# Start of a two-layer decoder step: loads split by the first chunk's needs, squares behind the raw chunks, norm sum inside block 1, products of zeros during the loads

## What is computed

```python
def rmsnorm(x, g):
    xf = x.astype(jnp.float32)
    y = xf * lax.rsqrt(jnp.mean(xf * xf, axis=-1, keepdims=True) + RMS_EPS)
    return (y * g.astype(jnp.float32)).astype(x.dtype)

def swiglu(h, w1, w3, w2):
    return (jax.nn.silu(h @ w1) * (h @ w3)) @ w2

h = rmsnorm(x, w['norm_ffn1'])
x = x + 0.5 * swiglu(h, w['ffn1_w1'], w['ffn1_w3'], w['ffn1_w2'])
...
lam = (jnp.exp(jnp.sum(w['lq1'] * w['lk1'])) - jnp.exp(jnp.sum(w['lq2'] * w['lk2'])) + lam_init)
```

## Time and profile before

| | |
|---|---|
| median of 3 runs | 2637.2 us (2636.78 to 2637.67) |
| profiled execution, own time | 2646.27 us |
| its span | 2644.4 us |
| TensorE busy | 2580.0 us (98%) |
| VectorE busy | 1793.3 us (68%) |
| ScalarE busy | 1188.8 us (45%) |
| mean granted TensorE clock | 0.992 of full |
| TensorE idle before its first product | 13.4 us |

### The profile page before, as it was taken

How to read it: one execution, slowest core, us unless ns; L and a number is a source line. 1 busy time by engine, 2 the same in 40 slices (tenths; PEclk the granted TensorE clock), 3 DMA queues, 4 the chain that set the end, 5 groups by cost and what they waited for, 6 DMA issues and landing times.

```text
span 2644.4 us, 54210 instructions
## 1 busy us (share of the span) xinstructions
PE 2580.0 (98%) x22900; PEld 2442.1 (92%) x22900; DVE 1793.3 (68%) x2307; ACT 1188.8 (45%) x1650; POOL 277.2 (10%) x150
## 2 busy tenths in 40 slices
PE   7999999999999999999999999999999999999997
PEld 7999999976699999999899999999757999999997
DVE  6887347655676798843798863567466758987346
ACT  5555223413663565532455542343236635555223
POOL 0102000331000010020001020013220000100200
PEclk9999999999999999999999999999999999999998
DMA  4233233278422233332223322322883222333221
GB/s 152 81 110 102 89 123 99 81 239 276 146 83 87 76 107 111 102 96 97 82 80 111 100 93 89 128 90 89 272 278 110 82 95 81 97 110 116 88 93 64
DMA packets 142110, 304.42 MB, mean 115 GB/s; under 512 B 14946, under 2 KB 25186, under 8 KB 141410
## 3 DMA queue, kind: packets, MB, share of 16 engines
q1 hardware_dynamic: 141922, 301.79, 34.5%
HBM read 290.30 MB, written 11.44 MB: 114 GB/s over the span
## 4 chain that ended last, share of the span: by engine, by line
PE 91%; DVE 5%; ACT 2%; DVEq 1%; issue 1%; DMA 0%; SPq 0%; ACTq 0%
PE ps L665 33%; PE ps L757 29%; PE ps L713 14%; PE ps L789 3%; PE ps L950 2%; PE ps L1042 1%; DVE ring L1944 1%; PE ps L1090 1%; PE ps L1105 1%; PE ps L1061 1%; PE ps L831 1%; PE ps L836 1%; PE ps L854 1%; PE ps L1259 1%; DVE pg L1944 0%
## 5 line engine op out<-in xcount | busy, mean ns | idle before, releaser
L665 PE MATMUL ps<-Gh,ring 128*128 128x260 f32 x2816 | 455.3, 283 | 5.9 <-DVE ring L1944 5.9
L665 PEld LDWEIGHTS ps<-Gh,ring 128*128 128x128 f32 x2816 | 387.1, 189 | 6.9 <-DVE ring L1944 6.9
L713 PE MATMUL ps<-Hh,ring 128*128 128x260 f32 x2048 | 342.3, 286 | 0.1
L1879 POOL TENSOR_TENSOR Gl<-G,Gh 128x520 fp32r<-128x520 f32 x88 | 151.2, 1740 | 1513.1 <-ACT Gh L1431 1513.1
L713 PEld LDWEIGHTS ps<-Hh,ring 128*128 128x128 f32 x2048 | 285.2, 188 | 4.3 <-issue 2.7
L665 PE MATMUL ps<-Gl,ring 128*128 128x260 f32 x1408 | 283.2, 283 | 0.0
L1944 DVE TENSOR_TENSOR ring<-rawd,ring 128x1408 fp32r<-128x1408 f32 x64 | 117.4, 1836 | 200.0 <-ACT ring L1431 200.0
L757 PE MATMUL ps<-HS,UHb 128*128 128x260 f32 x1280 | 234.3, 283 | 5.6 <-DVE ULb L1944 5.6
L757 PE MATMUL ps<-XR,UHa 128*128 128x260 f32 x1280 | 237.1, 283 | 0.0
L1431 ACT ACTIVATE ring<-raw 128x2048 fp32r<-128x2048 f32 (+1 forms) x72 | 134.3, 1866 | 227.0 <-PE ps L665 122.5
L1431 ACT ACTIVATE ring<-rawd 128x1408 fp32r<-128x1408 f32 x64 | 88.4, 1381 | 324.5 <-PE ps L665 319.7
(11 more groups left out here) (347 smaller groups left out, 5509.1 us busy)
## 6 DMA issues: line engine op xcount, KB each, us to landing
weven<-in_ffn_up SPq DMA_DIRECT2D x88, 512.0 KB, 4.7
wodd<-in_ffn_up SPq DMA_DIRECT2D x88, 512.0 KB, 4.8
rawd<-in_ffn_down SPq DMA_DIRECT2D x128, 352.0 KB, 3.5
kb<-in_cache_k SPq DMA_DIRECT2D x128, 256.0 KB, 4.2
kb<-in_cache_v SPq DMA_DIRECT2D x128, 256.0 KB, 3.9
raw<-in_w_in SPq DMA_DIRECT2D x56, 512.0 KB, 4.6
raw<-in_w_gate SPq DMA_DIRECT2D x32, 512.0 KB, 4.7
raw<-in_w_ab SPq DMA_DIRECT2D x16, 512.0 KB, 4.3
```

The lines of the kernel that those rows point to most:

```text
L665: last = nc.tensor.matmul(ps[:, bank + 2 * m + c, 0:HT], w, x[:, k0 + k, c * HT:(c + 1) * HT], start=starts and k == 0 and n == 0, stop=st ...
L713: last = nc.tensor.matmul(ps[:, 2 * m + c, 0:HT], w, x[:, k, c * HT:(c + 1) * HT], start=k == 0 and t == 0, stop=k == KD - 1 and t == 2)
L1879: nc.gpsimd.tensor_tensor(Gl[:, n, :], G0[:, n, :], Gh[:, n, :].bitcast(F32), ALU.subtract).then_inc(gl_done, 1)
```

## The change

Five edits, all at the start of layer 0's first FFN.

1. Block 0's weights go to `whole`, seven places of which four are used. The first DMA brings slots 0 and 3, those that chunk 0 needs, on a semaphore of its own; X chunks 0 and 1 follow, then slots 1 and 2 in a DMA each. ScalarE and VectorE split slots 0 and 3 ahead of raw chunk 0, and slots 1 and 2 behind it.
2. TensorE waits for the second half of block 0's split weights at chunk 1, no longer ahead of chunk 0. Later blocks wait as before.
3. All eight raw chunks are made first; the eight squares and their adds come behind them.
4. The norm sum is made inside block 1, ahead of its chunk 4, in columns 260 to 511 of banks 0 to 2, which no block uses, as three products (252, 252 and 16 columns). The root reads them with two activations. TensorE no longer waits for the root ahead of block 1.
5. VectorE clears a tile `warm`, and TensorE multiplies it with itself seven times (128 x 128 by 260 columns, fp32) ahead of block 0.

```diff
@@ def plain_parts
+            if n:
+                return WF[n % 2][q][:, 0:3:2, :], (UHa if w == 0 else ULa)[:, 2 * q:2 * q + 2, :] if n % 2 else (
+                    PWh[hid] if w == 0 else PWl[hid])[:, 2 * q:2 * q + 2, :]
+            s = (slice(0, 7, 6), slice(2, 5, 2))[q]
+            d = (slice(0, 4, 3), slice(1, 3))[q]
+            return whole[:, s, :], (PWh[hid] if w == 0 else PWl[hid])[:, d, :]
@@ up_load (SP), for block 0 of the later FFNs
+                if n == 0:
+                    s, d = ((slice(0, 4, 3), slice(0, 7, 6)), (slice(1, 3), slice(2, 5, 2)))[q]
+                    sp_.dma_start(whole[:, d, :], up[L, 0].rearrange("p (a c) -> p a c", a=4)[:, s, :]).then_inc(raw_ready[0], 16)
+                    return
@@ SP at the start
             sp_.dma_start(par[:, :], A["par"][:, 0:G_LAM]).then_inc(par_load, 16)
-            up_load(0, 0, A["ffn1_up"], 0, 0)
+            first = A["ffn1_up"][0, 0].rearrange("p (a c) -> p a c", a=4)
+            sp_.dma_start(whole[:, 0:7:6, :], first[:, 0:4:3, :]).then_inc(w_load, 16)
             x_in(0)
-            up_load(0, 0, A["ffn1_up"], 0, 1)
+            for q in range(1, 3):
+                sp_.dma_start(whole[:, 2 * q, :], first[:, q, :]).then_inc(raw_ready[0], 16)
@@ norm_sum (TensorE)
+                if L == 0 and nj == 0:
+                    for b, t in ((0, slice(0, 252)), (1, slice(252, 504)), (2, slice(504, T))):
+                        last = nc.tensor.matmul(ps[:, b, HT:HT + t.stop - t.start], ones, accu[:, t], start=True, stop=True)
+                    last.then_inc(sum_ready, 1)
+                    return
@@ up_plain (TensorE)
-                pe.wait_ge(split_done, n + (L * NB + nb + FREE + 1))
                 pe.wait_ge(evac, L * NE + n + (ub + 1))
                 for k in range(KD):
                     i, odd = divmod(k, 2)
+                    if k == (0 if n else 1):
+                        pe.wait_ge(split_done, n + (L * NB + nb + FREE + 1))
@@ ffn (TensorE)
+                def late_norm(k):
+                    if k == 4:
+                        norm_sum(L, nj)
+
                 up_plain(L, nb, ub, hid, 0, PWh[hid], PWl[hid], raw_part)
-                norm_sum(L, nj)
-                if np > 1:
-                    pe.wait_ge(rt_ready, L * NORMS + (nj + 1))
-                    for n in range(1, np):
-                        up_plain(L, nb, ub, hid, n, *((UHa, ULa) if n % 2 else (PWh[hid], PWl[hid])))
+                if np == 1:
+                    norm_sum(L, nj)
+                for n in range(1, np):
+                    up_plain(L, nb, ub, hid, n, *((UHa, ULa) if n % 2 else (PWh[hid], PWl[hid])), late_norm if n == 1 else None)
@@ TensorE, ahead of everything
+            pe.wait_ge(warm_ready, 1)
+            for n in range(7):
+                nc.tensor.matmul(ps[:, 7, 0:HT], warm[:, 0:P], warm[:, :], start=True, stop=True)
@@ norm_root (ScalarE)
+                if L == 0 and nj == 0:
+                    A_(R[:, 0:504].rearrange("p (a c) -> p a c", a=2), ps[:, 0:2, HT:512], ACT.Sqrt, scale=1.0 / D, bias=eps)
+                    A_(R[:, 504:T], ps[:, 2, HT:HT + 16], ACT.Sqrt, scale=1.0 / D, bias=eps).then_inc(rt_ready, 1)
+                    return
@@ ScalarE at the start
+            plain_high(0, 0, 0, 0, 0)
             for i in range(4):
                 act.wait_ge(x_load[i], 16)
                 if i == 0:
                     act.wait_ge(par_load, 16)
                 for m in (2 * i, 2 * i + 1):
                     raw_act(act, 0, 0, 0, m)
-                    if m < 2:
-                        plain_high(0, 0, 0, 0, m)
-                    else:
-                        square_act(act, 0, 0, m - 2)
-            for m in (KD - 2, KD - 1):
+                    if m == 0:
+                        plain_high(0, 0, 0, 0, 1)
+            for m in range(KD):
                 square_act(act, 0, 0, m)
@@ VectorE at the start
+            V.memset(warm[:, :], 0.0).then_inc(warm_ready, 1)
             V.memset(accu[:, :], 0.0)
+            plain_low(0, 0, 0, 0, 0)
+            for m in range(KD):
+                raw_dve(dve, 0, 0, 0, m)
+                if m == 0:
+                    plain_low(0, 0, 0, 0, 1)
             dve.drain()
             for m in range(KD):
-                raw_dve(dve, 0, 0, 0, m)
-                if m < 2:
-                    plain_low(0, 0, 0, 0, m)
-                else:
-                    square_dve(dve, 0, 0, m - 2)
-            for m in (KD - 2, KD - 1):
                 square_dve(dve, 0, 0, m)
```

More of the change, by code:

```diff
@@ L195, in hybrid_trunk @@
         weven = (at("weven", [P, 4, 512], F32, even_at), at("weven2", [P, 3, 512], F32, even_at + 8192))
+        whole = at("whole", [P, 7, 512], F32, even_at)
         assert even_at + 14336 <= top.at
@@ L208, in hybrid_trunk @@
         G0 = at("G0", [P, KF, T], F32, gl_at)
+        warm = at("warm", [P, HT], F32, gl_at + 20 * T * 4)
         accu = at("accu", [P, T], F32, tb_at + T * 4)
@@ L364, in hybrid_trunk @@
         VALUES = (1, 1, 1, 2, 1, 0, 1, 2, 1, 0, 1, 2, 0, 0, 0, 1, 1, 1)
-        loads, late_loads, par_load = sem("loads"), sem("late_loads"), sem("par_load")
+        loads, late_loads, par_load, w_load, warm_ready = (
+            sem(n) for n in ("loads", "late_loads", "par_load", "w_load", "warm_ready"))
         x_load = [sem(f"x_load{n}") for n in range(4)]
@@ L457, in formed, with plain_parts @@
             return sum(KF - plain(*f) for f in ((0, 0), (0, 1), (1, 0))[:2 * L + hid]) + n - plain(L, hid)
+        def plain_parts(hid, n, q, w):
+            if n:
[4 more added lines that the diff above has]
+            return whole[:, s, :], (PWh[hid] if w == 0 else PWl[hid])[:, d, :]
         def half_t(c):
@@ L1446, in plain_high @@
             def plain_high(L, nb, hid, n, q):
-                w = WF[n % 2][q]
-                to = UHa if n % 2 else PWh[hid]
-                act.wait_ge(raw_ready[n % 2], (L * NB + nb + n) // 2 * 32 + 32)
+                w, to = plain_parts(hid, n, q, 0)
+                if L or hid or n or q:
+                    act.wait_ge(raw_ready[n % 2], (L * NB + nb + n) // 2 * 32 + 32)
+                else:
+                    act.wait_ge(w_load, 16)
                 if n > 1:
                     act.wait_ge(block_done, L * NB + nb + n + 1)
-                A_(to[:, 2 * q:2 * q + 2, :], w[:, 0:3:2, :], ACT.Copy).then_inc(hi_done if q else up_hi, 1 if q else 2)
+                A_(to, w, ACT.Copy).then_inc(hi_done if q else up_hi, 1 if q else 2)
             def up_high(L, nb, hid, n, g):
@@ L1969, in plain_low @@
             def plain_low(L, nb, hid, n, q):
-                w = WF[n % 2][q]
-                h, l = (UHa, ULa) if n % 2 else (PWh[hid], PWl[hid])
+                (w, h), (w, l) = plain_parts(hid, n, q, 0), plain_parts(hid, n, q, 1)
                 if q:
@@ L1976, in plain_low @@
                     dve.wait_ge(up_hi, 2 * (up_first(L, hid) + n) + 2)
-                TT(l[:, 2 * q:2 * q + 2, :], w[:, 0:3:2, :], h[:, 2 * q:2 * q + 2, :].bitcast(F32), ALU.subtract
+                TT(l, w, h.bitcast(F32), ALU.subtract
                    ).then_inc(split_done if q else up_lo, 1 if q else 2)
```

## The result

The changed kernel takes 2645.27 us (median of 20 executions), the kernel before 2637.98 (20). The ratio is 1.0026, with a 95% interval of 1.0019 to 1.0033: 6.9 us slower, 5.0 to 8.7 (the two medians alone differ by 7.3). The direction was forecast, the size was not: 4.8 us and 2642.0 were said, with 2644.6 as the upper end. Of the 3.3 us between 2642.0 and 2645.27, 0.8 are before's own median, which was 2637.2 over 3 executions.

The account below looks back on a forecast made before the run. TensorE, busy 98%, was taken as the bound. Block 2 starting 3.2 us later plus 1.6 us of half clock in it gave 4.8 us on 2637.2, so 2642.0 us; range 2639.6 to 2644.6.

Parts of the forecast that it names:

- chunk 0 of block 0: TensorE's first chunk starts at about 9.2 us, once its half of the weights is split and X is there.
- end of the adds: VectorE's eight adds of squares, behind the raw chunks, end at 23.0 us, 0.9 sooner than 23.91.
- reciprocal: On VectorE, behind the late norm sum and root, it starts at 37.15 us instead of 29.16, 8.0 later.
- end of block 2's low parts: VectorE's PWl, queued behind the reciprocal, ends 8.26 us after the reciprocal's start; block 2 can't start without it.
- last form, behind before's: VectorE's last form, needed by TensorE at block 5, comes 4.95 us late after idle time is used up.
- The mechanism: Blocks 1 and 2 wait for ScalarE's and VectorE's chains: block 1 starts 1.4 us sooner, block 2 3.2 us later.
- The floor by VectorE's chain: At block 5, VectorE's late forms alone would make TensorE 4.5 us late, even with a cheaper second clock fall.
- The third rival: Block 1's split weights are ready when block 0 ends; block 2 starts 3.7 us sooner, 2633.5; chance 0.04.
- the term for the clock: Behind TensorE's waits before blocks 1 and 2 the clock falls to half, each fall costing 1.6 us.
- the first rival: Before's timed executions have no clock fall at block 1, so the change is 6.4 us slower, 2643.6; chance 0.2.
- a bound (2.4 of loss): Each of the two clock falls may lose 0.8 to 2.4 us, making the result +3.7 to +6.4.
- only the first 45 us or so: The part of the profiled execution that the diff was said to touch.

Follow-up runs that it names:

- Experiments 1: Changed kernel with the norm sum put back between blocks 0 and 1, still in the unused columns and without TensorE's wait for the root; ratio to before 0.9999.
- experiment 2: Kernel before with only the norm sum moved ahead of chunk 4 of block 1, in unused columns, no wait for the root; ratio 1.0017, 4.5 us.
- Experiments 5: Changed kernel with products of zeros filling TensorE's two new waits, eight ahead of block 1 and seven in its last chunk; ratio to before 1.0018.
- 7: Changed kernel with the split of block 2's weights moved ahead of the root on ScalarE and the reciprocal on VectorE; ratio to before 1.0018.
- Experiment 8: Changed kernel with block 1's weight split moved ahead of the squares and block 2's ahead of root and reciprocal; ratio to before 1.0002.
- experiment 3: Kernel before with only the eight squares and their adds moved behind all raw chunks; ratio 1.0003.
- experiment 11: Changed kernel with norm sum back between blocks 0 and 1, block 1's low parts on GpSimd, high copies between squares, lambda behind the root; ratio to before 1.0005.

## Why the prediction was right and where it was wrong

| step | said | profile |
|---|---|---|
| chunk 0 of block 0 | 9.2 | 10.54 |
| end of the adds | 23.0 | 23.01 |
| block 1 | 27.8 | 27.88 |
| norm sum | 35.1 | 35.23 |
| reciprocal | 37.15 | 37.28 |
| end of block 2's low parts | 45.4 | 45.54 |
| block 2 | 45.5 | 45.69 |
| end of block 2 | 58.6 | 58.80 |
| last form, behind before's | 4.95 | 5.00 |
| the loss, from the ratio | +4.8 | +6.9 |

- **The mechanism held throughout.** Block 1's start is set by ScalarE and VectorE, so the earlier start of TensorE buys 1.3 us of 2.9. The late sum puts the reciprocal 8.1 later, and everything queued behind it. Experiments 1 and 2 show it from both sides.
- **Chunk 0 was off by 1.3 us**, without effect. ScalarE's first table load had run under the wait for X in before; now it stands behind the wait for the weights:

```profile
5.91 1.28 ACT L1462 ACT_TABLE_LOAD   x1 [5.91 <-DMA whole<-in_ffn_up]
7.20 1.06 ACT L1462 ACTIVATE PWh<-whole 128x1024 fp32r<-128x1024 f32 x1
```

- **The floor by VectorE's chain was real.** It was called less than the 4.8 and a floor: in the changed kernel the last form ends at 81.61 + 1.24 = 82.85 and TensorE takes it at 83.29, with the same 0.45 of slack as in the earlier trace rows, so it did not hold TensorE up there. Experiments 5, 7 and 8 ran into it. The third rival (3.7 us faster) left this floor out: a reciprocal at 30.2 is 1.0 late, and 3.05 of idle time and 0.45 of slack give at most 2.5 us back at block 5. Experiment 8, with block 2 at 37.80, was only 1.7 sooner there than the earlier trace rows.
- **What failed is the term for the clock**, at both of its ends. The sum set two new falls of 1.6 us each against one fall in before. In before that fall was in the first profile, but in none of three more; in the changed kernel two of three profiles have a fall of 6.8 us at block 1. Taken over all profiles the difference is 7.2 instead of 5.0. Of these 2.2 us, 1.1 are the falls that before did not have, 0.7 the longer ones of the changed kernel, and 0.4 the scatter of block 1's start (28.63 to 29.23 before, 27.82 to 28.37 changed). The first half of this was the first rival, which was given 0.2 and 6.4 us: it deserved more, since the gap of before was the shortest, and a block 0 that stays longer at half clock shortens it below what the one profile had. The second half was in the text as a bound (2.4 of loss), yet the range added only part of it to that rival. With both, its upper end would have been 2637.2 + 8, and the time inside. That the timed executions have the same falls is argued from the agreement of 7.2 with 6.9, not seen: the 5.0 of the first two profiles also lies at the lower end of the measured 5.0 to 8.7.
- The loss of one fall of 3.4 us was sized well: block 1 took 35.23 - 27.88 = 7.35 us to the sum, for 5.76 at full clock, and block 2 13.1 for 11.5, so 1.6 each time. What was mis-sized is how many such stretches each kernel has, and that some are twice as long (block 1 to the sum took 8.20 and 8.51 us in the two new profiles).
- Two smaller slips. At 1.7 us for each of the two falls the sum gives 5.0, not the 4.9 that stands there. And the change does not touch "only the first 45 us or so": the starts of the second and fourth FFN cost some 0.7 us more, which the sum left out.

## What to carry to other kernels

Before moving a small reduction later, to hide it behind long work, list all that is queued behind its result on every engine: here 1.0 us of products was moved, which had run while TensorE had to wait anyway, and 8.3 us of reciprocal, read-out and splits slid behind it. Where a sum is made against one trace, ask of each term whether it would stand in a second trace; the fall of the clock after before's short gap did not. And when a wait is removed, look for the next engine's own chain over several blocks, not only for the next wait: it gave back 2.5 us twice.

## What the runs showed of the hardware

- The clock fell behind gaps of 1.86 and 1.96 us (before, and experiment 3, in which half clock ran from 30.06 for 3.4 us), and of 2.48 and 2.49 us (at block 5 in 7 and 8), and not behind gaps of 0.79, 1.18, 0.79 and 1.39 us (the three new profiles of before, experiment 2), nor behind one of 3.02 us (experiment 11). Every gap of 3.4 us or more ahead of block 1 or 2 in the changed kernel's three profiles had half clock behind it. At block 1 of the changed kernel the stretch at half was 3.4 us long in one profile and 6.8 in two. The Trainium skill's rule of thumb for the gaps to avoid ("TensorE: Matmul & The Clock Gate", section "HAM oscillation — how this bites in real kernels") would have let the gaps of 1.86 to 2.49 us pass; the measurement decides.
- The products of zeros reach the faster pace (each of their 14 passes took 0.44 us until 4.8 us, 0.22 from there on; the view's clock column reads 1.00 for both, so this is read from the passes), but 4.25 us of idle time follow and the clock was at half from 11.63.
- VectorE's add is held up beside GpSimd's subtraction, both with two inputs in SBUF: an add of 0.70 us took up to 2.73. Whether the subtraction is held up too, no run shows.
